# A decoder layer on one core: VectorE forms the second modulation set amid the attention output's tiles

## The chip, the core and the metric

The kernel runs on 1 core of one Trainium2 chip. The metric is the device time of one execution in microseconds (us). TensorE multiplies matrices into PSUM banks, VectorE and ScalarE do elementwise work, GpSimd a little, and SyncE's queue issues nearly all the weight loads; each engine takes its own instructions in order and waits for the others on semaphores.

## The reference

One layer with a mixer (a convolution branch and an attention branch) and a sparse expert stage. What matters here, cut down (D_MODEL is 1024, 256 tokens):

```python
mod = (c_act @ w_ada[l] + b_ada[l])[:, None, :]
shift1, scale1, gate1, shift2, scale2, gate2 = jnp.split(mod, 6, axis=-1)
h = rms_norm(x, norm1_g[l]) * (1.0 + scale1) + shift1
x = x + gate1 * mixer(h, ...)      # q, k, v, conv, gates; attention; w_conv_out, w_attn_out, w_o
h = rms_norm(x, norm2_g[l]) * (1.0 + scale2) + shift2
x = x + gate2 * moe(h, w_router[l], ...)      # top 4 of 32 experts
```

`mod` is one row of 6 x 1024 numbers from a 1024 x 6144 matrix in f32: 24 MB of weights for one row. The experts' weights are 32 x 12 MB.

## The kernel before

**Three modulation sets.** The first set (shift1, scale1) is made at the start. The second (columns 2048 to 4095 of `w_ada`: gate1 and shift2) and the third (scale2 and gate2) are each four blocks of 2 MB, `ADA0[0]` and `ADA0[1]`. The second is formed on TensorE: `ada_rows` (L1267) multiplies all four blocks with the activated `c`, 32 products of 512 columns, each of which the trace shows as two instructions. The third is formed on VectorE: `mod_product(k)` (L885, L887) adds one eighth of the weights, scaled by one number for each partition, to a running sum of 128 x 2048; it starts amid attention head 5 (`MOD_AT`), and `sum_rows` (L1403) on TensorE adds the 128 partitions with four products by ones. `ada_row(gi)` (L877) adds the bias and leaves the row in `modrow2`. ScalarE's queue then sends `modrow2` by 12 small DMAs into `gate1` and `gate2` (inside `u_conv`), spread over the partitions (`mod_ready` counts to 16 x 12). `turn_rows(gi)` (L1393) transposes the row for shift2 or scale2, and VectorE keeps it in `mod2` (L1012, L1094), from which the router's weights are made (L1102 to L1105).

**The ring of weight blocks.** The weights ahead of the experts go through a ring of 6 places (`RING`), 2 MB each. `blocks` lists them in order of loading; block n is loaded by L487 when block n - 6 is used up (`used`). Before the change the order after the first convolution blocks is: second set (4), q and k (4), v (2), gates (4), third set (4), w_conv_out (2), w_attn_out (2), w_o (2).

**The expert slots.** The same memory is 12 slots of 2 MB for the experts: each expert has 6 chunks (4 of `w_up`, 2 of `w_down`), so 12 slots hold two experts. `SLOT_ORDER` says which slot chunk i takes; a slot is free when the mixer's tile or ring block that lay there is done with, and SyncE's stream (L467) waits for each of these ends in turn. Chunks (0,0) to (1,5) are loaded during the mixer and the routing; every later one waits until `chunk_used` tells that expert e - 2 has used its chunk.

**The mixer on TensorE.** In order: the convolution's columns (L1353), the second set (L1267), q and k (8 tiles) and v (4 tiles) at L1361, `turn_rows(0)`, transposes of q and k (L1416), eight heads with the gates' projections between (L1368), `conv_out` 0 to 2, `sum_rows`, transposes of the attention output (L1499), `conv_out(3)`, `turn_rows(1)`, the four tiles of `y_attn` (L1368), the four of `w_o` (L1520), transposes of the new x (L1529), the router, then the expert units. VectorE works on the depthwise convolution (L917, 496 instructions, dealt out between other steps by hand), on q and k, on the heads, and at the end on `y_attn` (L1112, L1114) and in `add_branch` (L1122, L1123), which multiplies a `w_o` tile by `gate1` and adds it to x.

**The four PSUM banks.** `order` numbers the uses of the four banks; use n lies in bank n % 4, and `fill` lets TensorE into it only when VectorE or ScalarE has freed use n - 4.

Of the kernel before, what the change touches and what calls it, by code (L numbers as in the profile page):

```python
# [59 lines left out]
SLOT_ORDER = (HEAD_SLOT, 0, VALUE_SLOT, 1, ROW_SLOT, 2, 3, CONV_SLOT, GATE_SLOT, 4, 5, SMALL_SLOT)  # L60
# [13 lines left out]
def build(nc, x, c, positions, w_ada, b_ada, norm1_g, w_in, conv_w, conv_b, conv_ln_g, conv_ln_b,  # L74
# [3 lines left out]
    with ctx:  # L78
# [28 lines left out]
        def small(shape, dt=F32):  # L107
# [142 lines left out]
        c_ready, ada_done, xT_done = (sem(n) for n in ("c_ready", "ada_done", "xT_done"))  # L250
# [21 lines left out]
        mod_ready, ebias_ready, conv_sum, tables_kept, mod_summed, last_rows, in_cols2 = (  # L272
            sem(n) for n in ("mod_ready", "ebias_ready", "conv_sum", "tables_kept", "mod_summed", "last_rows", "in_cols2"))
# [19 lines left out]
        ADA0 = [len(blocks), 0]  # L293
        blocks += [ada_block(4 * NB, i) for i in range(4)]
# [11 lines left out]
        blocks += [block_of(w_attn_out, 0), block_of(w_attn_out, NB)]  # L306
        WO0 = len(blocks)
# [44 lines left out]
        order += [("ada", 0)] + [("qk", i) for i in range(8)]  # L352
        order += [("v", i) for i in range(4)] + [("mod2T", 0)] + [("qkT", i) for i in range(8)]
# [13 lines left out]
        order += [(name, i) for name in ("y_attn", "w_o") for i in range(4)]  # L367
# [12 lines left out]
        WO_USE = use_of["w_o", 0]  # L380
# [21 lines left out]
        for i in range(3):  # L402
            used[ADA0[0] + i] = (ada_done, i + 1)
            used[ADA0[1] + i] = (mod_summed, 2 * i + 3)
# [5 lines left out]
        for i in range(2):  # L410
# [4 lines left out]
            used_by(WO0 + i, WO_USE + 2 + i)  # L415
# [23 lines left out]
        def _(sp):  # L439
# [34 lines left out]
            for n, src in enumerate(blocks):  # L474
# [15 lines left out]
            sp.wait_ge(*used[COUT0])  # L490
            load_chunk(0, 1)
            full(sp, OT_USE + 3)
            load_chunk(0, 2)
            sp.wait_ge(*used[COUT0 + 1])
            load_chunk(0, 3)
            sp.wait_ge(mod_ready, 16 * 12)
            full(sp, M2T_USE[1])
            sp.wait_ge(ebias_ready, 3 * PARTS)
            load_chunk(0, 4)
            sp.wait_ge(*used[AOUT0])  # L500
            load_chunk(0, 5)
            sp.wait_ge(*used[AOUT0 + 1])
            load_chunk(1, 0)
            full(sp, YA_USE + 3)
            load_chunk(1, 1)
            sp.wait_ge(mixed, 4)
            load_chunk(1, 2)
# [316 lines left out]
        def _(dve):  # L824
# [198 lines left out]
            for h in range(HEADS):  # L1023
# [40 lines left out]
                if h >= MOD_AT:  # L1064
                    mod_product(h - MOD_AT)
# [651 lines left out]
```

## Time and profile before

| | us |
|---|---|
| median of 3 runs | 1262.33 |
| lowest, highest | 1262.19, 1263.87 |
| the profiled execution | 1263.07 |
| its span (first to last instruction) | 1261.2 |
| TensorE busy | 1079.8 (86%) |
| VectorE busy | 417.5 (33%) |
| ScalarE busy | 221.1 (18%) |
| moved by DMA | 475.80 MB, mean 377 GB/s |

The page gives the whole span in 40 slices of 31.5 us. Two stages are to be told apart: up to about 350 us the mixer and the routing, where TensorE is at nine or ten tenths, and from there the experts, where the DMA stream stands at 426 to 429 GB/s. Times "at" in the text are us from the span's start.

### The profile page before, as it was taken

Reading aid. Unit: us, or ns where it says so; the run is one execution under the profiler, and the core shown is the slowest. Engines: PE = TensorE matmul, PEld = TensorE weight load, DVE = VectorE, ACT = ScalarE, POOL = GpSimd, SP = SyncE. Lnnn points to the kernel's source line nnn. Section 1 sums busy time; section 2 is a strip of 40 time slices with the busy share of each in tenths; the row PEclk is TensorE's granted clock in tenths of the full one; section 3 lists DMA queues with packets and bytes.
Section 4 is the critical chain, followed back from the end, with each engine's and each line's share of the span. In section 5 each row is a group of like instructions: output and inputs, shape, how many; then the busy total and the mean of one; then the engine's idle time right before and its main releaser. Section 6 shows DMA issues by size and latency. Waiting matters only on the chain.

```text
span 1261.2 us, 23331 instructions
## 1 busy us (share of the span) xinstructions
PE 1079.8 (86%) x9898; PEld 527.8 (42%) x9898; DVE 417.5 (33%) x1122; ACT 221.1 (18%) x462; POOL 46.0 (4%) x74
## 2 busy tenths in 40 slices
PE   8999999999998766569998668979669696999995
PEld 5864468888442222124443223423224232444431
DVE  1489997762331111113222112312112121223221
ACT  2111133640220101001111001101002111112110
POOL 2000000451000000000000000000000000000000
PEclk9999999999998888889999879979889788999998
DMA  9999353499799999999999999999999999799997
GB/s 329 339 371 361 133 171 134 158 348 347 302 365 428 428 426 427 428 427 428 427 427 428 427 426 429 427 428 427 427 429 426 428 427 428 305 424 428 426 426 321
DMA packets 66491, 475.80 MB, mean 377 GB/s; under 512 B 6417, under 2 KB 20182, under 8 KB 39670
## 3 DMA queue, kind: packets, MB, share of 16 engines
q1 hardware_dynamic: 62676, 472.54, 91.4%
q10 hardware_dynamic: 3746, 2.21, 0.6%
q8 instruction: 58, 0.95, 0.3%
q14 instruction: 11, 0.09, 0.0%
HBM read 473.03 MB, written 1.05 MB: 376 GB/s over the span
## 4 chain that ended last, share of the span: by engine, by line
PE 47%; DMA 31%; SPq 16%; ACT 2%; DVE 2%; issue 1%; another core or an unknown queue 0%; ACTq 0%; DVEq 0%
DMA weights<-in_w_down 25%; SPq L467 15%; PE bank L1651 13%; PE bank L1681 7%; PE bank L1368 7%; PE bank L1361 7%; DMA weights<-in_w_up 4%; PE bank L1297 2%; PE bank L1520 2%; PE bank L1592 2%; DMA weights<-in_w_in 2%; PE bank L1579 2%; PE bank L1353 1%; PE bank L1599 1%; DMA weights<-in_w_ada 1%; ACT buf_d L815 1%
## 5 line engine op out<-in xcount | busy, mean ns | idle before, releaser
L1651 PE MATMUL bank<-weights,buf_d 128*32 128x512 f32 x3008 | 392.8, 669 | 124.7 <-DMA weights<-in_w_up 124.7
L1651 PEld LDWEIGHTS bank<-weights,buf_d 128*32 128x32 f32 x3008 | 96.5, 117 | 388.8 <-DMA weights<-in_w_up 193.0
L1681 PE MATMUL bank<-weights,buf_d 128*32 128x256 f32 x3008 | 185.5, 395 | 42.1 <-DMA weights<-in_w_down 39.2
L1238 DVE TENSOR_SCALAR u_conv<-bank 128x256 f32<-128x256 f32 x47 | 20.0, 425 | 449.2 <-PE bank L1651 449.2
L1681 PEld LDWEIGHTS bank<-weights,buf_d 128*32 128x32 f32 x3008 | 93.2, 113 | 119.1 <-DMA weights<-in_w_down 50.2
L811 ACT ACTIVATE u_conv<-u_conv 128x256 f32<-128x256 f32 x47 | 19.6, 416 | 696.9 <-DVE u_conv L1238 696.9
L917 DVE SCALAR_TENSOR_TENSOR weights<-u_conv,weights 128x256 f32<-128x256 f32 x240 | 97.8, 480 | 0.5
L1361 PE MATMUL bank<-weights,buf_d 128*128 128x512 f32 x192 | 82.7, 593 | 0.1
L1250 DVE TENSOR_TENSOR buf_d<-bank,u_conv 128x256 f32<-128x256 f32 x47 | 20.0, 425 | 187.4 <-PE bank L1681 187.4
L811 ACT ACT_TABLE_LOAD x47 | 60.3, 1283 | 1.4 <-issue 0.6
L1368 PE MATMUL bank<-buf_d,weights 128*128 128x256 f32 x256 | 58.1, 380 | 0.0
L1592 PE MATMUL bank<-buf_d 32*128 32x256 f32 x768 | 57.6, 415 | 0.6 <-DVE buf_d L1250 0.6
L1592 PEld LDWEIGHTS bank<-buf_d 32*128 32x128 f32 x768 | 36.5, 195 | 48.0 <-issue 46.5
L1368 PE MATMUL bank<-weights 128*128 128x256 f32 x256 | 55.9, 379 | 0.0
L1361 PEld LDWEIGHTS bank<-weights,buf_d 128*128 128x128 f32 x192 | 36.4, 190 | 46.4 <-issue 45.4
L1368 PEld LDWEIGHTS bank<-weights 128*128 128x128 f32 x256 | 48.3, 190 | 6.4
L1368 PEld LDWEIGHTS bank<-buf_d,weights 128*128 128x128 f32 x256 | 47.4, 190 | 6.4 <-issue 0.7
L1579 PE MATMUL bank<-x_tok,u_conv 128*32 128x256 f32 x768 | 50.0, 380 | 0.0
L1585 PE MATMUL bank<-ident,buf_d 128*128 128x128 f32 x190 | 38.2, 309 | 0.2 <-ACT buf_d L804 0.2
L1599 PE MATMUL bank<-late,u_conv 96*32 96x256 bf16 (+1 forms) x376 | 34.2, 349 | 0.5 <-DVE buf_d L1200 0.5
L1585 PEld LDWEIGHTS bank<-ident,buf_d 128*128 128x128 f32 x190 | 30.0, 204 | 4.3 <-ACT buf_d L804 0.3
L1199 DVE TENSOR_TENSOR buf_d<-bank,u_conv 128x256 f32<-128x256 f32 x48 | 20.4, 424 | 32.1 <-PE bank L1585 32.1
(276 smaller groups left out, 806.5 us busy)
## 6 DMA issues: line engine op xcount, KB each, us to landing
weights<-in_w_up SPq DMA_DIRECT2D x128, 2048.0 KB, 38.9
weights<-in_w_down SPq DMA_DIRECT2D x63, 2048.0 KB, 44.0
weights<-in_w_in SPq DMA_DIRECT2D x10, 2048.0 KB, 17.5
weights<-in_w_ada SPq DMA_DIRECT2D x8, 2048.0 KB, 13.2
weights<-in_w_ada SPq DMA_DIRECT2D x8, 1024.0 KB, 11.4
weights<-in_w_in SPq DMA_DIRECT2D x8, 512.0 KB, 9.2
weights<-in_w_in SPq DMA_DIRECT2D x4, 1024.0 KB, 13.9
weights<-in_w_conv_out SPq DMA_DIRECT2D x2, 2048.0 KB, 8.0
```

The source lines that it names most:

```text
L467: sp.dma_start(dst, src).then_inc(w_full[chunk_slot(e, j)], 16)
L811: s.activation(sg, glu, ACT.Sigmoid, scale=ALPHA).then_inc(sg_ready, 1)
L917: ins = v.scalar_tensor_tensor(acc, u_conv[:, k, w:w + T], tap(k, w), acc, ALU.mult, ALU.add)
L1297: ins = t.matmul(PS[4 + k][:, T * half:T * half + T], first_conv(i)[:, kk, half, P * k:P * k + P], h1T[:, 2 * i + kk, :], start=False, sto ...
L1361: ins = t.matmul(bank(use)[:, :], lhsT[:, k, P * tt:P * tt + P], blk(n)[:, k, :], start=(k == 0), stop=(k == KD - 1))
L1368: ins = t.matmul(bank(use)[:, T * j:T * j + T], blk(n)[:, k, at:at + P], rhs[:, k, :], start=(k == 0), stop=(k == KD - 1))
L1579: ins = t.matmul(GX[SLOTS * g:SLOTS * g + SLOTS, 0:T], pick[:, tt, :], x_tok[:, tt, T * g:T * g + T], start=(tt == 0), stop=(tt == TT - 1))
L1585: ins = t.transpose(bank_[:, at + P * r:at + P * r + P], src.rearrange("p (c r) -> p r c", r=2)[:, r, :], ident[:])
L1592: ins = t.matmul(Y[q][:, T * tt:T * tt + T], Cmb[rows, P * tt:P * tt + P], oe[rows, :], start=False, stop=True, skip_group_check=True)
L1599: t.matmul(bank_[SLOTS * g:SLOTS * g + SLOTS, 0:width], sel, rows(g), start=True, stop=False)
L1651: ins = t.matmul(UP[SLOTS * g:SLOTS * g + SLOTS, :], xgT[:, r, SLOTS * j:SLOTS * j + SLOTS], up_group(w[:, r, :], g), start=False, stop=(j ...
L1681: ins = t.matmul(DOWN[rows, 0:T], actT[:, r, at:at + SLOTS], w[:, g, r, T * q:T * q + T], start=False, stop=(h == 1 and g == 1 and r == 1))
```

## The change

- TensorE no longer forms the second set: `ada_rows` and the wait for `ada_done` are gone. `mod_product` takes the set as an argument, and VectorE forms the second set too, two products behind each of the four `y_attn` tiles. `sum_rows(0)` comes behind the second `w_o` tile, `turn_rows(0)` behind the third.
- The four blocks of the second set are loaded behind `w_attn_out` and ahead of `w_o`.
- `ada_row(0)`, and with it the 12 small DMAs of `gate1` and `gate2`, comes after the last `y_attn` tile on VectorE; the router's weights are made between the second and the third `add_branch`.
- `SLOT_ORDER` and the waits between the early expert chunks are others; GpSimd's split of the expert biases waits for the second set's last product, no longer the third's.

```diff
-SLOT_ORDER = (HEAD_SLOT, 0, VALUE_SLOT, 1, ROW_SLOT, 2, 3, CONV_SLOT, GATE_SLOT, 4, 5, SMALL_SLOT)
+SLOT_ORDER = (HEAD_SLOT, VALUE_SLOT, 0, 1, 2, CONV_SLOT, GATE_SLOT, 3, 4, ROW_SLOT, 5, SMALL_SLOT)
...
-        ADA0 = [len(blocks), 0]
-        blocks += [ada_block(4 * NB, i) for i in range(4)]
+        ADA0 = [0, 0]
         QK0 = len(blocks)
...
         blocks += [block_of(w_attn_out, 0), block_of(w_attn_out, NB)]
+        ADA0[0] = len(blocks)
+        blocks += [ada_block(4 * NB, i) for i in range(4)]
         WO0 = len(blocks)
...
-        order += [(name, i) for name in ("y_attn", "w_o") for i in range(4)]
+        order += [("y_attn", i) for i in range(4)]
+        order += [("w_o", 0), ("w_o", 1), ("ada", 0), ("w_o", 2), ("mod2T", 0), ("w_o", 3)]
...
+                if n == WO0:
+                    full(sp, OT_USE + 3)
+                    load_chunk(0, 1)
+                    sp.wait_ge(*used[ADA0[0]])
+                    load_chunk(0, 2)
+                if n == WO0 + 1:
+                    sp.wait_ge(*used[ADA0[0] + 1])
+                    load_chunk(0, 3)
                 sp.wait_ge(*used[n - RING])
...
-            pool.wait_ge(mod_summed, KD)
+            pool.wait_ge(mod_summed[0], KD)
...
             glu_tile(7)
-            ada_row(0)
             conv(1, 0, 8)
...
                 v.tensor_tensor(mixT[:, 2 * i:2 * i + 2, :], m, ga, ALU.add).then_inc(mixed, 1)
+                for k in (2 * i, 2 * i + 1):
+                    mod_product(0, k)
+            ada_row(0)
+
+            dve.wait_ge(mod_ready, 16 * 12)
...
+            add_branch(0, 0)
+            add_branch(0, 1)
+            full(dve, M2T_USE[0])
+            v.tensor_copy(by_chunk[:, 0, :, :, :], columns(0, 2)).then_inc(bank_free[M2T_USE[0] % 4], 1)
...
-            fill(pe, ADA_USE[0])
-            for i in range(4):
-                ada_rows(ADA_USE[0], ADA0[0], i)
...
                 ins.then_inc(bank_full[use % 4], 1)
+                if i == 1:
+                    sum_rows(0)
+                if i == 2:
+                    turn_rows(0)
```

What SyncE issues from the second half of w_conv_out on, before (each row a load; `in_w_up` and `in_w_down` are expert chunks):

```order
L487 DMA weights<-in_w_conv_out 128x8x512 [waits bank_full3]
L487 DMA weights<-in_w_attn_out 128x8x512 [waits mod_summed] x2
L487 DMA weights<-in_w_o 128x8x512 [waits mod_summed]
L487 DMA weights<-in_w_o 128x8x512 [waits bank_full3]
L467 DMA weights<-in_w_up 128x4096 [waits bank_full1]
L467 DMA weights<-in_w_up 128x4096 [waits bank_full3]
L467 DMA weights<-in_w_up 128x4096 [waits bank_full0]
L467 DMA weights<-in_w_down 128x4096 [waits ebias_ready,bank_full1,mod_ready]
L467 DMA weights<-in_w_down 128x4096 [waits bank_full3]
L467 DMA weights<-in_w_up 128x4096 [waits bank_full1] x2
L467 DMA weights<-in_w_up 128x4096 [waits mixed]
```

and now:

```order
L498 DMA weights<-in_w_conv_out 128x8x512 [waits bank_full1]
L498 DMA weights<-in_w_attn_out 128x8x512 [waits mod_summed1] x2
L498 DMA weights<-in_w_ada 128x2x2048 [waits mod_summed1]
L498 DMA weights<-in_w_ada 128x2x2048 [waits bank_full1]
L498 DMA weights<-in_w_ada 128x2x2048 [waits bank_full3]
L498 DMA weights<-in_w_ada 128x2x2048 [waits bank_full2]
L470 DMA weights<-in_w_up 128x4096 [waits bank_full1]
L470 DMA weights<-in_w_up 128x4096 [waits mod_summed0]
L498 DMA weights<-in_w_o 128x8x512 [waits bank_full1]
L470 DMA weights<-in_w_up 128x4096 [waits mod_summed0]
L498 DMA weights<-in_w_o 128x8x512 [waits bank_full3]
L470 DMA weights<-in_w_down 128x4096 [waits mod_summed0]
```

Four loads of `w_ada` and three expert chunks now stand ahead of the second load of `w_o`, and the first of `w_o` waits no longer for a product of the third set but for a bank that TensorE fills in `y_attn`.

TensorE from the second `w_o` tile to the transposes of x, before:

```order
L1520 MATMUL bank<-weights,buf_d 128x512 [waits blk_full5,bank_free3]
L1520 MATMUL bank<-weights,buf_d 128x512 x7
L1520 MATMUL bank<-weights,buf_d 128x512 [waits bank_free0]
L1520 MATMUL bank<-weights,buf_d 128x512 x7
L1520 MATMUL bank<-weights,buf_d 128x512 [waits bank_free1]
L1520 MATMUL bank<-weights,buf_d 128x512 x7
L1529 MATMUL bank<-ident,x_tok 128x128 [waits bank_free2]
L1529 MATMUL bank<-ident,x_tok 128x128 x3
```

and now (L1517 is `w_o`, L1401 `sum_rows(0)`, L1391 `turn_rows(0)`, L1530 the transposes of x):

```order
L1517 MATMUL bank<-weights,buf_d 128x512 [waits blk_full5,bank_free1]
L1517 MATMUL bank<-weights,buf_d 128x512 x7
L1401 MATMUL bank<-weights 32x512 [waits mod_summed0,bank_free2]
L1401 MATMUL bank<-weights 32x512 x3
L1517 MATMUL bank<-weights,buf_d 128x512 [waits bank_free3]
L1517 MATMUL bank<-weights,buf_d 128x512 x7
L1391 MATMUL bank<-ident,weights 128x128 [waits bank_free2,bank_free0]
L1391 MATMUL bank<-ident,weights 128x128 x3
L1517 MATMUL bank<-weights,buf_d 128x512 [waits bank_free1]
L1517 MATMUL bank<-weights,buf_d 128x512 x7
L1530 MATMUL bank<-ident,x_tok 128x128 [waits bank_free2]
L1530 MATMUL bank<-ident,x_tok 128x128 x3
```

By the kernel's own list `order`, `turn_rows(0)` has the bank of the first `w_o` tile, and the last `w_o` tile that of the second, so both now stand behind an `add_branch`.

VectorE at the last `y_attn` tile, before (L1112 and L1114 the tile, L1122 and L1123 `add_branch`):

```order
L1112 TENSOR_TENSOR weights<-weights,bank 128x512 [waits bank_full1]
L1114 TENSOR_TENSOR buf_d<-weights 128x512 [waits bank_free1]
L1122 TENSOR_TENSOR bank<-bank,u_conv 128x512 [waits bank_full2,mod_ready]
L1123 TENSOR_TENSOR x_tok<-x_tok,bank 128x512 [waits dve_step]
L1122 TENSOR_TENSOR bank<-bank,u_conv 128x512 [waits bank_full3]
L1123 TENSOR_TENSOR x_tok<-x_tok,bank 128x512 [waits dve_step]
```

and now (L1105 and L1107 the tile, L891 `mod_product`, L883 `ada_row(0)`, L1118 and L1119 `add_branch`):

```order
L1105 TENSOR_TENSOR weights<-weights,bank 128x512 [waits bank_full3]
L1107 TENSOR_TENSOR buf_d<-weights 128x512 [waits bank_free3]
L891 SCALAR_TENSOR_TENSOR weights<-weights 128x2048 [waits mod_summed0,blk_full3]
L891 SCALAR_TENSOR_TENSOR weights<-weights 128x2048 [waits mod_summed0]
L883 TENSOR_TENSOR weights<-bank,weights 128x512 [waits bank_full2,in_rows2]
L1118 TENSOR_TENSOR bank<-bank,u_conv 128x512 [waits bank_full0,mod_ready]
L1119 TENSOR_TENSOR x_tok<-x_tok,bank 128x512 [waits dve_step]
```

Between the last tile and the first `add_branch` two products and the bias row have come in, and the wait for `mod_ready` is now for DMAs that can only start behind that row.

## Rows read from the trace of the kernel before

**Rows 1.** The page, part 2: the DMA rate in 40 slices.
```profile
GB/s 329 339 371 361 133 171 134 158 348 347 302 365 428 428 426 427 428 427 428 427 427 428 427 426 429 427 428 427 427 429 426 428 427 428 305 424 428 426 426 321
```
**Rows 2.** Windows: busy time of each engine, granted clock, DMA share, GB/s.
```profile
core 0: us, PE busy (x) PEld busy (x) DVE busy (x) ACT busy (x) POOL busy (x), PEclk, DMA share, GB/s
345.00:350.00 5.00, 4.04 (x36) 1.94 (x34) 4.30 (x21) 1.93 (x9) 0.00 (x0) 1.00 0.21 39
...
1090.00:1100.00 10.00, 9.94 (x142) 4.88 (x135) 3.03 (x8) 2.72 (x5) 0.00 (x0) 1.00 0.39 165
1100.00:1110.00 10.00, 9.94 (x110) 3.93 (x106) 2.99 (x11) 1.35 (x4) 0.00 (x0) 1.00 0.76 287
```
**Rows 3.** Timeline of SyncE's issues: start, duration, line, tiles, count.
```profile
262.49 11.16 SPq L487 DMA_DIRECT2D weights<-in_w_o  x2
...
337.63 11.24 SPq L467 DMA_DIRECT2D weights<-in_w_down  x2
354.62 5.48 SPq L467 DMA_DIRECT2D weights<-in_w_up  x4
```
**Rows 4.** Timeline of TensorE: start us, us, line, shapes, count.
```profile
80.94 7.07 PE L1267 MATMUL bank<-weights 128*32 128x512 f32 x64
...
187.78 0.52 PE L1425 MATMUL bank<-ident,weights 128*128 128x128 f32 x3
...
272.16 1.06 PE L1403 MATMUL bank<-weights 128*32 128x512 f32 x8
...
309.97 27.63 PE L1520 MATMUL bank<-weights,buf_d 128*128 128x512 f32 x64
...
351.37 8.34 PE L1651 MATMUL bank<-weights,buf_d 128*32 128x512 f32 x64
```
**Rows 5.** Timeline of VectorE from the convolution to the first head.
```profile
86.06 0.42 DVE L892 TENSOR_TENSOR u_conv<-bank,weights 128x256 f32<-128x256 f32 x1
88.15 0.69 DVE L877 TENSOR_TENSOR weights<-bank,weights 128x512 f32<-128x512 f32 x1 [1.67 <-PE bank L1267]
88.76 0.73 DVE L914 TENSOR_SCALAR weights<-u_conv,weights 128x256 f32<-128x256 f32 x2
...
171.41 0.17 DVE L1012 COPY weights<-bank 128x8 f32<-128x8 f32 x1
171.53 8.13 DVE L917 SCALAR_TENSOR_TENSOR weights<-u_conv,weights 128x256 f32<-128x256 f32 x20
...
187.16 0.48 DVE L1044 SCALAR_TENSOR_TENSOR weights<-weights 128x256 f32<-128x256 f32 x1
```
**Rows 6.** Timeline of VectorE: products, bias row, y_attn tiles, add_branch.
```profile
232.34 1.28 DVE L887 TENSOR_SCALAR weights<-weights 128x2048 f32<-128x2048 f32 x1
...
252.69 7.18 DVE L885 SCALAR_TENSOR_TENSOR weights<-weights 128x2048 f32<-128x2048 f32 x3
...
273.37 0.69 DVE L877 TENSOR_TENSOR weights<-bank,weights 128x512 f32<-128x512 f32 x1 [0.22 <-PE bank L1403]
...
296.36 0.69 DVE L1112 TENSOR_TENSOR weights<-weights,bank 128x512 f32<-128x512 f32 x1 [5.42 <-PE bank L1368]
...
310.89 0.69 DVE L1114 TENSOR_TENSOR buf_d<-weights 128x512 f32<-128x512 f32 x1
...
338.44 0.69 DVE L1123 TENSOR_TENSOR x_tok<-x_tok,bank 128x512 f32<-128x512 f32 x1
```
**Rows 7.** Two expert chunks issued at 301.5 and 301.9: issue to landing.
```profile
DMA to landing us min/median/max: 7.7/9.9/12.2
```
**Rows 8.** The 12 small DMAs of modrow2: issue, and issue to landing.
```profile
L613 ACTq DMA_DIRECT2D u_conv<-weights x12: 604/612/635, 275.2 to 282.3; - x12
...
DMA to landing us min/median/max: 5.8/13.4/19.2
```
**Rows 9.** DMA queues from 287 to 290: packets, MB, share (q10 is ScalarE's).
```profile
q1 hardware_dynamic: 83, 1.13, 99.2%
q10 hardware_dynamic: 83, 0.08, 7.9%
```
**Rows 10.** Timeline of TensorE, 16 instructions behind 1.24 and 2.97 us idle.
```profile
397.77 1.93 PE L1651 MATMUL bank<-weights,buf_d 128*32 128x512 f32 x16 [1.24 <-DMA weights<-in_w_up]
402.67 3.64 PE L1651 MATMUL bank<-weights,buf_d 128*32 128x512 f32 x16 [2.97 <-DMA weights<-in_w_up]
```

More of the change, by code:

```diff
@@ L351, in build @@
         order = [("conv", i) for i in range(4, 8)]
[L352 to L353 removed]
+        order += [("qk", i) for i in range(8)]
+        order += [("v", i) for i in range(4)] + [("qkT", i) for i in range(8)]
         for h in range(HEADS):
@@ L379, in build @@
         YA_USE = use_of["y_attn", 0]
-        WO_USE = use_of["w_o", 0]
+        WO_USE = [use_of["w_o", i] for i in range(4)]
         M2T_USE = [use_of["mod2T", i] for i in range(2)]
@@ L402, in build @@
         for i in range(3):
-            used[ADA0[0] + i] = (ada_done, i + 1)
-            used[ADA0[1] + i] = (mod_summed, 2 * i + 3)
+            for gi in range(2):
+                used[ADA0[gi] + i] = (mod_summed[gi], 2 * i + 3)
         for i in (2, 3):
@@ L1095, in _, with add_branch @@
                 bank_free[M2T_USE[1] % 4], 1)
+            dve.wait_ge(gate_ready, 2)
+            for i in range(4):
+                use = YA_USE + i
+                full(dve, use)
+                m = gates[:, 2 * i:2 * i + 2, :]
+                ga = gates[:, KD + 2 * i:KD + 2 * i + 2, :]
+                v.tensor_tensor(ga, ga, bank(use)[:, :].rearrange("p (c t) -> p c t", t=T), ALU.mult).then_inc(bank_free[use % 4], 1)
+                freed(dve, use)
+                v.tensor_tensor(mixT[:, 2 * i:2 * i + 2, :], m, ga, ALU.add).then_inc(mixed, 1)
+                for k in (2 * i, 2 * i + 1):
+                    mod_product(0, k)
+            ada_row(0)
+            dve.wait_ge(mod_ready, 16 * 12)
+            def add_branch(tt, half):
+                use = WO_USE[2 * tt + half]
+                cs = slice(NB * half, NB * half + NB)
+                full(dve, use)
+                step(v.tensor_tensor(bank(use)[:, :], bank(use)[:, :], gate1[:, cs], ALU.mult))
+                v.tensor_tensor(x_tok[:, tt, cs], x_tok[:, tt, cs], bank(use)[:, :], ALU.add).then_inc(bank_free[use % 4], 1)
+            add_branch(0, 0)
+            add_branch(0, 1)
+            full(dve, M2T_USE[0])
+            v.tensor_copy(by_chunk[:, 0, :, :, :], columns(0, 2)).then_inc(bank_free[M2T_USE[0] % 4], 1)
             dve.wait_ge(in_moe, 16)
@@ L1105, in _ @@
             v.tensor_tensor(wr[:], wr[:], mod2[:, 1, :].unsqueeze(2).to_broadcast([P, KD, EXPERTS]), ALU.mult).then_inc(ws_ready, 1)
[L1106 to L1126 removed]
+            add_branch(1, 0)
             dve.wait_ge(h_sq, 3)
@@ L1260, in wait_block @@
                 pe.wait_ge(blk_full[place(n)], 16 * loads_before[n])
-            def ada_rows(use, n0, i):
-                wait_block(n0 + i)
-                for k in (2 * i, 2 * i + 1):
-                    for gi in range(4):
-                        ins = t.matmul(bank(use)[32 * gi:32 * gi + 32, :], c_act[:, k, :], blk(n0 + i, 2)[:, k % 2, NB * gi:NB * gi + NB],
-                                       start=(k == 0), stop=(k == KD - 1))
-                ins.then_inc(*((ada_done, 1) if i < 3 else (bank_full[use % 4], 1)))
             def mod_row(i):
```

101 lines of the change are left out of this document (38 added, 63 removed).

## Prediction, made before the changed kernel was run

> **What bounds the kernel now.** Read the page's second part first, the DMA rate in 40 slices [rows 1]. From the slice at 378 us on nearly all stand at 426 to 429 GB/s, so from there the experts' weights set the pace; before that the rate is far lower, so something else does. The windows and SyncE's timeline tell where the one stage passes into the other. Just before the first unit the DMA does next to nothing (39 GB/s from 345 to 350) [rows 2]: all 12 slots are filled or on their way, the last by the load issued about 348.5, and the next load goes out only at 354.62 [rows 3], when the first expert unit, begun at 351.37 [rows 4], has used its first chunk. From there 180 chunks follow at the DMA's rate. So the end is that moment plus a fixed stream, and every us by which the first unit comes earlier or later is a us of the total. What precedes the first unit is TensorE's chain through the mixer; so I ask how that chain moves.
>
> **Removed from TensorE: 7.07 us, of which 2.5 count.** The 64 instructions at L1267 take 80.94 to 88.0 [rows 4]. They go, and q and k can start at 81. But VectorE is as busy there. Its L892 ends at 86.48; it then waits 1.67 us for TensorE and spends 0.69 us on the bias row, and the next convolution step starts at 88.76 instead of about 86.4 [rows 5]. That is 2.35 us. From there to the first head VectorE is a chain of its own; with the copy at 171.41, which leaves 0.12 us by the starts of two rows [rows 5], its chain gains 2.5 us. It ends the first head's probabilities at 187.64 [rows 5], and TensorE takes them up at 187.78 [rows 4], so the two are level there today. TensorE would be there 7.5 us earlier and must wait about 5 of them. Front: **-2.5 us** (the bound on the other side is -7.5, if VectorE were not in the way).
>
> **Added on VectorE amid y_attn: nothing on the path.** One plain product is 1.28 us, the others 7.18 / 3 = 2.39 [rows 6]; two a tile are at most 4.8, and a tile's own two steps 1.4. VectorE idles 5.42 us ahead of such a tile [rows 6], so a period is 6.9 us and 6.2 are now filled. If the products were 0.7 us dearer, the tiles would slip. The third product ends at 296.36 - 2.5 + 1.4 + 2.4 = 297.7, the fifth 6.9 later at 304.6, the seventh at 311.58 - 2.5 + 2.4 = 311.5, the eighth at 313.9. The blocks themselves are in time: TensorE's use of the conv output and sums lets the last be issued by about 280.
>
> **w_o's weights come late: two waits.** Today both are issued at 262.5 and 273.3, well ahead of 309.97 [rows 3, 4]. Now expert chunk (0,2) waits for the third product (297.7) and the first w_o load stands behind it, at 298.2. Of two loads in a row the second lands 12.2 us after its issue, the first 7.7 [rows 7], so 2 MB more cost about 4.9 with the 0.4 between the issues; w_o's rows are short, and I add 0.4. First w_o block: 298.2 + 12.6 = 310.8. TensorE is there at 309.97 - 2.5 = 307.5, waits 3.3, and the tile (27.63 / 4 = 6.9 [rows 4]) ends at 317.7. The second w_o load needs y_attn's end (307.5), behind chunk (0,3), issued at 304.6: queue 310.8 + 4.8 = 315.6, and 5.4 more gives 321.0. TensorE waits 3.3 again. After idling 2.97 us the granted clock was at its lower level: 16 instructions took 3.64 us instead of 1.93 [rows 10]. I add 1.7 for the second tile (0 to 3.4), and it ends at 321.0 + 6.9 + 1.7 = 329.6; today, less the 2.5, it would end at 321.2. So these waits cost **+8.4 us**.
>
> **gate1 comes late: the largest term.** Then `sum_rows(0)`, 1.06 us [rows 4], the bias row 0.69 [rows 6] and two handovers of 0.1: 331.6. ScalarE issues the 12 small DMAs from 331.8, at 0.61 to 0.64 each [rows 8], the last at 338.9. Landing is the unknown: 5.8 to 19.2 us in the trace [rows 8], with expert chunks in flight then as now. While both queues have work, they move equal numbers of packets, 83 and 83 in 3 us [rows 9], although one queue's are some 14 times as big: a small packet waits its turn behind a chunk's. Here chunks (0,4) to (1,0) go out at about 312, when queued behind w_o land one in some 4.8 us, to 335.4; (1,1) follows `sum_rows` (331) and lands at about 341; (1,2) follows the third w_o tile (338) and lands at about 347. Then the big queue is empty, since (1,3) now waits for `mod_ready`, and the rest of the small packets get through in some 3.5 us. I take **350.5**, nearer to the middle of the landings (338.9 + 11.6) than to either end; the bounds are 338.9 + 5.8 = 344.7 and 338.9 + 19.2 = 358.1.
>
> **Behind it.** Today VectorE handles a w_o tile as soon as TensorE is done, and the last `add_branch` ends at 339.13 [rows 6]. Now nothing is added before 350.7. Two `add_branch` of 1.4 end at 353.6. Only then may TensorE start the last w_o tile, since its bank is that of the second (the order of instructions shows the wait). It has idled some 12 us by then, so it starts at the lower clock: 6.9 + 2.5 (1.3 to 3.4; the first unit of today took 8.34 us for a stage that is 7.0 at the full clock) [rows 4, 10]. It ends at 363.0, and the last `add_branch` at 364.5. The copy for shift2, the router's weights (2.8 us) and the third `add_branch` fit beside that tile. From the last `add_branch` to the first unit the work is today's, 12.2 us (339.13 to 351.37). GpSimd's split of the biases, 24 us from 313.9, ends at about 338 and keeps nobody waiting.
>
> **Sum.** 364.5 - 339.1 = +25.4 us; by parts: -2.5 front, +8.4 w_o's waits, +19.5 for sum, row, DMAs and the last tile behind them. Profiled execution 1263.07 + 25.4 = 1288.5; the median stands 0.7 below that execution, so **1288 us**, 2% slower. Its own range, from the landing's bounds (-6, +7.5) and the clock's (-4, +2.5), mostly not together, is 1281 to 1296.
>
> **Rivals.** *The small DMAs land quickly.* For: some landed within 5.8 us [rows 8]. Against: the median was 13.4. Time: 344.7 instead of 350.5, 1282. The Trainium skill, "DMA: Bandwidth & Descriptors", section on queues, rings and completion order, says that a DMA engine changes from one queue to the next only after a whole packet of some 9 to 17 descriptors. If that held for what the profile counts, the small writes would leave many at a turn and this rival would be the forecast, 1282; the equal counts in the rows speak against it.
>
> *They land slowly.* For: the 12 small DMAs were under way from 275.2 to 282.3 + 19.2 = 301.5, some 26 us [rows 8]. Placed behind 331.8 they end at 358. Against: the chunks run dry at 347 this time. Time: 1288 + 7.5 = 1296.
>
> *TensorE's whole saving counts.* Were VectorE not level with it in the first head, the front would be -7.5, and the total 1283; VectorE's rows speak against it [rows 5].
>
> *The delay is absorbed, and it isn't slower.* Mechanism: the expert stream makes up later what the first unit loses, so that only the front's -2.5 is left: 1260. It needs some 28 us of idle DMA behind the start. The only hole inside is at 1090 to 1110, where 165 and 287 GB/s instead of 428 leave 6.1 + 3.3 = 9.4 us [rows 2], and there TensorE is busy 9.94 of 10 us: it is TensorE's own stretch, which shifts along. The mechanism decides only if the DMA were still filling slots when the first unit starts; it was idle.
>
> **Chances.** Forecast 0.50, quick landing 0.23 (with smaller waits for w_o also below 1281), slow landing 0.14, whole saving 0.09, absorbed 0.04. The forecast's range with most of the two landings gives 1278 to 1297. A change of 0.2% (2.5 us) is about what can be told from none in this kernel. Faster 0.02, within 0.2% 0.02, slower 0.96.
>
> **What would show it.** In the profile of the changed kernel: q and k start at 81; the first head's probabilities are taken up near 185; TensorE idles about 3 us ahead of each of the first two w_o tiles, on `in_w_o`; VectorE's first `add_branch` waits for a DMA of `u_conv` until about 350; the last w_o tile starts behind the second `add_branch`; the first unit starts near 377 and the stream behind it has today's length. It is wrong if the last `add_branch` ends before 355, if the small DMAs land before TensorE is done with the third w_o tile (338), or if the first unit comes late and the end doesn't.

## The result, and the profile after

| | before | after |
|---|---|---|
| median, us | 1262.81 (4 runs, 1262.19 to 1263.87) | 1291.84 (4 runs, 1290.09 to 1293.04) |
| profiled execution, us | 1263.07 | 1292.84 |
| its span, us | 1261.2 | 1290.9 |
| last `add_branch` ends, us from the start | 339.13 | 367.50 |
| first expert unit starts | 351.37 | 379.60 |
| last weight load issued | 1211.91 | 1239.57 |

The kernel became 2.25% slower: the ratio is 1.0225, with a 95% interval from 1.0213 to 1.0237. The forecast was 1288 us with a range of 1278 to 1297. The last three lines of the table tell most of it: 28.4 us are lost before the last `add_branch` and none is given back: at the last weight load 27.7 are left. The remaining 2 us of this execution lie at the very end, where the last piece of `w_down` let TensorE wait 2.85 us instead of 1.34 and the instructions behind it ran at a lower clock; the medians differ by 29.0.

The profile's page, part 2, of the kernel after: the two lines for the granted clock and the DMA rate (40 slices, now of 32.3 us), answers to [rows 1]:

```profile
PEclk9999989998899788879999888988989898999998
...
GB/s 326 335 319 184 173 73 127 222 369 318 348 241 428 428 427 426 428 428 427 427 426 428 427 428 427 428 427 428 425 429 427 426 428 427 316 411 427 426 427 295
```

The reader should see two things. From the 13th slice on the DMA line is the old one: 426 to 429 GB/s, with the same dip near the end. And the slice before it, from 355 us, stands at 241, where the old profile had 365. The windows of the kernel after (columns as in [rows 2]) open up the hole:

```profile
180.00:190.00 10.00, 4.84 (x15) 3.74 (x14) 9.79 (x29) 3.47 (x15) 0.00 (x0) 0.69 0.00 0
190.00:200.00 10.00, 10.00 (x55) 8.24 (x54) 8.27 (x19) 2.92 (x11) 0.00 (x0) 0.97 0.55 210
345.00:350.00 5.00, 0.00 (x0) 0.00 (x0) 0.00 (x0) 0.00 (x0) 0.00 (x0) 0.50 0.91 350
350.00:355.00 5.00, 0.00 (x0) 0.00 (x0) 1.31 (x3) 0.00 (x0) 0.00 (x0) 0.50 0.20 74
```

From 345 to 350 no engine computes, only the DMA works; from 350 to 355 hardly that. The two windows at 180 matter below.

TensorE's timeline of the kernel after, answering to [rows 4] (start, duration, line, shapes, count, and in brackets the idle time ahead with what ended it):

```profile
81.38 19.05 PE L1362 MATMUL bank<-weights,buf_d 128*128 128x512 f32 x44
...
185.76 0.87 PE L1422 MATMUL bank<-ident,weights 128*128 128x128 f32 x3 [5.16 <-DVE weights L1047]
186.43 5.69 PE L1369 MATMUL bank<-buf_d,weights 128*128 128x256 f32 x16
...
282.70 27.79 PE L1369 MATMUL bank<-weights 128*128 128x256 f32 x128
314.70 9.89 PE L1517 MATMUL bank<-weights,buf_d 128*128 128x512 f32 x16 [4.21 <-issue]
325.09 7.10 PE L1517 MATMUL bank<-weights,buf_d 128*128 128x512 f32 x16 [0.49 <-DMA weights<-in_w_o]
332.12 1.06 PE L1401 MATMUL bank<-weights 128*32 128x512 f32 x8
333.12 7.13 PE L1517 MATMUL bank<-weights,buf_d 128*128 128x512 f32 x16
355.13 1.13 PE L1391 MATMUL bank<-ident,weights 128*128 128x128 f32 x4 [14.88 <-DVE x_tok L1119]
356.46 9.51 PE L1517 MATMUL bank<-weights,buf_d 128*128 128x512 f32 x16 [0.20 <-DVE x_tok L1119]
```

And VectorE's, answering to [rows 6], with the 12 small DMAs behind its bias row, answering to [rows 8]:

```profile
303.63 0.69 DVE L1105 TENSOR_TENSOR weights<-weights,bank 128x512 f32<-128x512 f32 x1 [0.85 <-PE bank L1369]
...
311.87 4.73 DVE L891 SCALAR_TENSOR_TENSOR weights<-weights 128x2048 f32<-128x2048 f32 x2
333.33 0.69 DVE L883 TENSOR_TENSOR weights<-bank,weights 128x512 f32<-128x512 f32 x1 [16.73 <-PE bank L1401]
353.65 0.70 DVE L1118 TENSOR_TENSOR bank<-bank,u_conv 128x512 f32<-128x512 f32 x1 [19.63 <-DMA u_conv<-weights]
```
```profile
L620 ACTq DMA_DIRECT2D u_conv<-weights x12: 604/612/630, 334.1 to 341.2; - x12
...
DMA to landing us min/median/max: 7.0/9.4/12.5
```

SyncE's timeline of the kernel after, the two loads of `w_o`, answering to [rows 3]:

```profile
300.81 0.43 SPq L498 DMA_DIRECT2D weights<-in_w_o  x1
...
310.53 0.38 SPq L498 DMA_DIRECT2D weights<-in_w_o  x1
```

Read in order of time, the chain of the loss is all there. TensorE is through with `y_attn` at 310.5, finds no weights and stands for 4.21 us (the profile puts it down to "issue", but the load went out only at 300.81, where it used to go out at 262.5); `sum_rows(0)` comes at 332.12 behind the second `w_o` tile; VectorE, with its products done since 316.6, adds the bias at 333.33; ScalarE sends the row out from 334.1; the first `add_branch` gets it at 353.65; and TensorE, out of work since 340.3, may begin the last `w_o` tile at 356.46, at half clock.

### The profile page after: what moved, and what is told of

It is laid out like the page before. It is cut to its first block, busy times and chain, and to the rows that moved or that the text cites. A ratio compares the mean times of both kernels' runs of the same rounds, so it can differ in the third digit from the quotient of the medians.

```text
span 1290.9 us, 23231 instructions
## 1 busy us (share of the span) xinstructions
PE 1082.4 (84%) x9842; PEld 529.1 (41%) x9842; DVE 432.2 (33%) x1130; ACT 220.0 (17%) x462; POOL 43.7 (3%) x74
## 4 chain that ended last, share of the span: by engine, by line
PE 33%; DMA 30%; SPq 15%; DVE 12%; issue 5%; ACT 3%; ACTq 1%; another core or an unknown queue 0%; DVEq 0%
DMA weights<-in_w_down 24%; SPq L470 15%; PE bank L1652 13%; DVE weights L923 7%; PE bank L1682 7%; DMA weights<-in_w_up 4%; PE bank L1369 3%; PE bank L1298 2%; PE bank L1593 2%; PE bank L1580 1%; DMA u_conv<-weights 1%; DMA weights<-in_w_ada 1%; PE bank L1600 1%; PE bank L1517 1%; ACT buf_d L822 1%
## 5 line engine op out<-in xcount | busy, mean ns | idle before, releaser
L1682 PE MATMUL bank<-weights,buf_d 128*32 128x256 f32 x3008 | 179.8, 386 | 37.5 <-DMA weights<-in_w_down 34.6
L818 ACT ACTIVATE u_conv<-u_conv 128x256 f32<-128x256 f32 x47 | 19.6, 417 | 693.9 <-DVE u_conv L1247 693.9
L1362 PE MATMUL bank<-weights,buf_d 128*128 128x512 f32 x192 | 82.6, 592 | 0.0
L1259 DVE TENSOR_TENSOR buf_d<-bank,u_conv 128x256 f32<-128x256 f32 x47 | 19.9, 424 | 177.1 <-PE bank L1682 177.1
L1593 PE MATMUL bank<-buf_d 32*128 32x256 f32 x768 | 60.3, 431 | 0.6 <-DVE buf_d L1259 0.6
L1517 PE MATMUL bank<-weights,buf_d 128*128 128x512 f32 x64 | 33.6, 686 | 4.9 <-issue 4.2
L891 DVE SCALAR_TENSOR_TENSOR weights<-weights 128x2048 f32<-128x2048 f32 x14 | 33.3, 2381 | 0.3
```

Of the source, the lines that this page charges most:

```text
L818: s.activation(sg, glu, ACT.Sigmoid, scale=ALPHA).then_inc(sg_ready, 1)
L1362: ins = t.matmul(bank(use)[:, :], lhsT[:, k, P * tt:P * tt + P], blk(n)[:, k, :], start=(k == 0), stop=(k == KD - 1))
L1517: ins = t.matmul(bank(use)[:, :], mixT[:, k, P * tt:P * tt + P], blk(n)[:, k, :], start=(k == 0), stop=(k == KD - 1))
L1593: ins = t.matmul(Y[q][:, T * tt:T * tt + T], Cmb[rows, P * tt:P * tt + P], oe[rows, :], start=False, stop=True, skip_group_check=True)
L1682: ins = t.matmul(DOWN[rows, 0:T], actT[:, r, at:at + SLOTS], w[:, g, r, T * q:T * q + T], start=False, stop=(h == 1 and g == 1 and r == 1))
```

## The experiments

All ratios are to the kernel before, run beside it on the same chip. Edits are shown against the changed kernel, that of the front experiment against the kernel before.

**The quiet queue.** Is gate1 late because small DMAs are slow, or because expert chunks are in the way? Here SyncE doesn't load chunks (1,1) and (1,2) until the small DMAs have landed.

```diff
             sp.wait_ge(*used[ADA0[0] + 3])
+            sp.wait_ge(mod_ready, 16 * 12)
             load_chunk(1, 1)
             sp.wait_ge(*used[WO0])
             load_chunk(1, 2)
-            sp.wait_ge(mod_ready, 16 * 12)
```

> The changed kernel, but chunks (1,1) and (1,2) are held back until the 12 small DMAs have landed. Theory: the last small DMA lands some 6 to 7 us after its issue at 341, the first add_branch starts near 348 instead of 353.65, and the total falls by 5 to 6 us, to about 1286.5. Rival (fixed landing time, whatever else is in flight): unchanged, 1291.8.

Measured: 1283.02 us, ratio 1.0152 (1.0135 to 1.0169), against 1.0225 of the change. The landings of the 12 small DMAs and the first `add_branch` in this kernel:

```profile
DMA to landing us min/median/max: 1.9/2.9/4.4
```
```profile
344.56 0.70 DVE L1118 TENSOR_TENSOR bank<-bank,u_conv 128x512 f32<-128x512 f32 x1 [10.77 <-DMA u_conv<-weights]
```

With the same 12 DMAs, issued from 333.9 instead of 334.1 on, the landing falls from 9.4 to 2.9 us in the median, and the first `add_branch` comes 9.1 us sooner. So about 9 us of the change are chunks in the way, more than the 5 to 6 that the theory gave them. What is left of the wait, 10.8 us, is mostly ScalarE's issuing of 12 DMAs at 0.61 each. The chunks held back cost nothing: the first unit starts 9.9 us earlier (369.68), and the span is 9.7 us shorter.

**w_o first.** Both loads of `w_o` are put ahead of the chunks (0,2) and (0,3); the waits for `w_o` should shrink. The rival says that the us won there are lost again on gate1.

```diff
                     load_chunk(0, 1)
-                    sp.wait_ge(*used[ADA0[0]])
-                    load_chunk(0, 2)
-                if n == WO0 + 1:
-                    sp.wait_ge(*used[ADA0[0] + 1])
-                    load_chunk(0, 3)
...
-            sp.wait_ge(*used[ADA0[0] + 2])
-            load_chunk(0, 4)
+            for i in range(3):
+                sp.wait_ge(*used[ADA0[0] + i])
+                load_chunk(0, 2 + i)
```

> The changed kernel, but both w_o loads go out ahead of expert chunks (0,2) and (0,3). The second w_o tile should start about 318 instead of 325.1, 6.9 us earlier. Theory (the small DMAs of gate1 share the queues packet by packet with the expert chunks): the chunks held back are then in flight beside the small DMAs, these still land near 351, and the total falls by 2 to 4 us only, to 1288 to 1290. Rival (the small DMAs take a fixed 12.5 us from their issue): the whole 6.9 us arrive in the total, 1285.

Measured: 1294.98 us, ratio 1.0246 (1.0229 to 1.0263), not faster than the change; whether it is slower, the overlapping intervals don't tell. Both expectations, 1288 to 1290 and 1285, were too low. Its first two `w_o` tiles on TensorE, its first `add_branch`, and its small DMAs:

```profile
310.76 7.03 PE L1513 MATMUL bank<-weights,buf_d 128*128 128x512 f32 x16
318.91 7.11 PE L1513 MATMUL bank<-weights,buf_d 128*128 128x512 f32 x16 [1.13 <-DMA weights<-in_w_o]
```
```profile
356.61 0.70 DVE L1114 TENSOR_TENSOR bank<-bank,u_conv 128x512 f32<-128x512 f32 x1 [28.77 <-DMA u_conv<-weights]
```
```profile
L616 ACTq DMA_DIRECT2D u_conv<-weights x12: 605/612/635, 327.9 to 335.0; - x12
...
DMA to landing us min/median/max: 6.5/14.1/21.6
```

The second tile is over 6.2 us sooner than in the changed kernel and the small DMAs go out 6.2 us sooner, and yet the last one lands 3 us later, 21.6 us after its issue. A wait on the path was removed and another took over its whole length. How the two queues share the DMA can be read off their packets (q1 is SyncE's, q10 ScalarE's), here from 345 to 349 us of this kernel, and then from 343 to 347 of the changed one, where the big queue has gaps up to 345:

```profile
q1 hardware_dynamic: 90, 1.38, 92.7%
q10 hardware_dynamic: 90, 0.13, 9.8%
```
```profile
q1 hardware_dynamic: 72, 0.92, 67.1%
q10 hardware_dynamic: 262, 0.30, 31.7%
```

As in [rows 9], both queues move equal numbers of packets, 90 and 90, while both are full; once the big one has gaps, the small one moves 262 to its 72. So the last small DMA lands at about the time at which the chunks run dry: the last chunk ahead of the first `add_branch`, (1,2), landed at 352.4 us in the changed kernel and at 357.3 here, the last small DMA at 353.7 and 356.6. Why the chunks run dry later here, although (1,2) is issued 6.2 us sooner, the windows tell: with `w_o` first, SyncE holds chunks (0,2) and (0,3) back, and the DMA moves 172 GB/s instead of 317 from 300 to 310 us and 305 instead of 408 from 310 to 320, against 270 instead of 217 from 290 to 300. That is 2.0 MB less, or 4.6 us of stream, and (1,2) lands 4.9 us later. The Trainium skill, "DMA: Bandwidth & Descriptors", section "Queues, rings and completion order", has the engine drain a packet of some 9 to 17 descriptors before it changes to the next queue. The equal counts and the 14.1 us in the median show no such advantage for the queue of small writes; whether what the profile counts as a packet is what that page means by one, no run here shows.

**A warm front.** In the changed kernel TensorE waits 5.16 us ahead of the first head, and the 16 instructions behind it take 5.69 us. Is that the clock, and does it matter? 26 products of constants, whose result nobody reads, fill the gap.

```diff
                 fill(pe, use)
+                if h == 0:
+                    for _ in range(26):
+                        t.matmul(bank(use)[:, 0:384], identb[:], maskb[:], start=True, stop=True, skip_group_check=True)
                 pe.wait_ge(pa_ready, h + 1)
```

> The changed kernel, with 26 idle products of 384 columns in bf16 (some 5 us) in the bank of the first head's transposes, in the 5.16 us that TensorE otherwise idles there. Theory (the front's 2.5 us were lost to the lower granted clock behind that idle time): the projection behind it takes 3.6 us instead of 5.69, y_attn starts near 280 instead of 282.7, total about 1289.0. Rival (something else ate the front's gain): no gain, 1291.8.

Measured: 1287.53 us, ratio 1.0195 (1.0178 to 1.0212). The same place in this kernel, then the 16 instructions in the kernel before (its transposes stand in [rows 4]):

```profile
185.38 0.55 PE L1425 MATMUL bank<-ident,weights 128*128 128x128 f32 x3 [0.80 <-DVE weights L1047]
185.76 3.62 PE L1369 MATMUL bank<-buf_d,weights 128*128 128x256 f32 x16
```
```profile
188.14 3.62 PE L1368 MATMUL bank<-buf_d,weights 128*128 128x256 f32 x16
```

TensorE takes up the first head 2.4 us earlier than before, as forecast, and now keeps them: `y_attn` starts at 279.99, against 282.34 before and 282.70 in the change. So the idle time at the first head did no harm by itself; the clock behind it ate the whole gain of the front. The first unit starts 4.3 us earlier than in the change, 2.7 of that from the front; both loads of `w_o` also land 1.1 us sooner after their issue (why, no run shows), and the last tile takes 8.99 us instead of 9.51.

**Both together.** If the two losses are independent, their gains add.

> The changed kernel with both edits that helped it alone: chunks (1,1) and (1,2) held back until the small DMAs have landed (1283.0), and the 26 idle products in the first head (1287.5 against 1291.8). If the two causes are apart, the gains add: 1283.0 - 4.3 = 1278.7. If they are one, it stays near 1283.

Measured: 1276.68 us, ratio 1.0110 (1.0094 to 1.0125). The ratio is 1.15 points below the change's; the single edits gave 0.73 and 0.30, and their sum is 1.03. The first unit starts at 364.83, 14.8 us earlier than in the change, where the single edits gave 9.9 and 4.3. Within the intervals the gains add, so the two losses are independent.

**gate1 early.** How much is the whole way of gate1 worth, with the bank of the last `w_o` tile? The small DMAs send the memory of the row before it is formed, and VectorE forms `ada_row(0)` behind the wait. So gate1 is not computed; the router then chooses other experts, with other numbers of units, and the total can't be compared, only the time up to the first unit.

```diff
-            for gi in range(2):
-                act_e.wait_ge(bank_free[ADA_USE[gi] % 4], ADA_USE[gi] // 4 + 1)
+            act_e.wait_ge(bank_free[ADA_USE[1] % 4], ADA_USE[1] // 4 + 1)
...
-            ada_row(0)
             dve.wait_ge(mod_ready, 16 * 12)
+            ada_row(0)
```

> The changed kernel with the formed gate1 left out: its 8 DMAs send the bias row alone, as early as before the change, so no add_branch waits for a late DMA; all products, sums and loads stay. Theory (gate1's way through the DMAs, and the last w_o tile behind it, is the largest term): the last w_o tile ends near 347.7 instead of 366, the last add_branch near 349.3 instead of 367.5, total 18 us lower, about 1273.6. Rival (w_o's late weights are the main cost): a fall of under 8 us, above 1284.

Measured: the first unit at 360.81, 18.8 us before the change's (total 1266.77). The waits for `w_o` are untouched, and the last tile starts right behind the third:

```profile
314.14 9.64 PE L1515 MATMUL bank<-weights,buf_d 128*128 128x512 f32 x16 [4.31 <-issue]
324.53 7.11 PE L1515 MATMUL bank<-weights,buf_d 128*128 128x512 f32 x16 [0.76 <-DMA weights<-in_w_o]
...
340.00 7.03 PE L1515 MATMUL bank<-weights,buf_d 128*128 128x512 f32 x16
```

That is the third term of the sum, measured nearly alone: 19.5 in the forecast. Of the 18.8 here 0.6 are already there at the second `w_o` tile (324.53 instead of 325.09); the other 18.2 and the 1.06 us of `sum_rows`, which stays in this kernel, make 19.3.

**The front alone.** In the kernel before, each block of the second set takes one product instead of eight, and nothing else changes. 28 of 32 products are left out, so gate1 and shift2 are wrong, and the router's choices and the number of units with them; only the time up to the first unit is comparable.

```diff
-                for k in (2 * i, 2 * i + 1):
-                    for gi in range(4):
-                        ins = t.matmul(bank(use)[32 * gi:32 * gi + 32, :], c_act[:, k, :], ...)
+                ins = t.matmul(bank(use)[32 * i:32 * i + 32, :], c_act[:, i, :], ...)
```

> The kernel before, with 28 of the 32 products that form the second modulation set left out (4 remain, so that every wait stays); nothing else is moved. Theory (VectorE is level with TensorE in the first head, and the idle time there costs clock): VectorE gains about 1.6 us, TensorE idles some 4 us ahead of the first head's transposes and loses about 2 to the lower clock, total 1262.5 to 1263.8, no gain. Rival 1 (no loss by the clock): about 1261. Rival 2 (the whole 6.2 us count): about 1256.6.

Measured: the first unit at 354.31, 2.9 us later than before (total 1272.32). TensorE behind the products:

```profile
80.89 1.40 PE L1265 MATMUL bank<-weights 128*32 128x512 f32 x8
88.32 11.98 PE L1359 MATMUL bank<-weights,buf_d 128*128 128x512 f32 x21 [6.03 <-DMA weights<-in_w_in]
```

My reason for the front falls in this kernel: it is not VectorE that TensorE waits for, but the weights of q and k, which are loaded behind the four blocks of the second set, the first of them from 67.2 on. The first lands at 88, just as the products used to end. In the changed kernel these loads start at 46.5, and q and k start at 81.38. SyncE's timeline, in the kernel before and in the changed one (from the first block of q and k on):

```profile
67.22 33.13 SPq L487 DMA_DIRECT2D weights<-in_w_in  x6
```
```profile
46.49 21.41 SPq L498 DMA_DIRECT2D weights<-in_w_in  x4
```

So removing the products from TensorE alone gives nothing; it is the other half of the edit, the order of the blocks, that opens the front (no run moves the blocks alone). And behind 6.03 us of idling the 192 instructions of q, k and v take 85.4 us instead of 82.7 (the granted clock is 0.70 and 0.62 in the two windows of 5 us from 85 on), which is nearly all of the 2.9 lost. The theory had VectorE as the reason and the wait at the first head, where this kernel has none.

**The swap.** Must the set with gate1 be the late one? Here gate1 and shift2 are formed amid the heads, and scale2 and gate2, needed only later, amid `y_attn`; gate2 gets four small DMAs and a count of its own.

```diff
-        ADA0[1] = len(blocks)
-        blocks += [ada_block(8 * NB, i) for i in range(4)]
+        ADA0[0] = len(blocks)
+        blocks += [ada_block(4 * NB, i) for i in range(4)]
...
-            ada_row(0)
-
-            dve.wait_ge(mod_ready, 16 * 12)
+
+            dve.wait_ge(mod_ready, 16 * 8)
...
             add_branch(0, 1)
-            full(dve, M2T_USE[0])
+            ada_row(1)
+            full(dve, M2T_USE[1])
```

> The changed kernel with the two late sets exchanged: the set with gate1 is formed amid the heads, the one with scale2 and gate2 amid y_attn, and gate2 has a semaphore of its own. Nothing is left out. Theory (gate1's late arrival is worth some 18 us, w_o's late weights some 8): the last add_branch ends near 349.5, total about 1273.5. Rival (the set's late place itself costs, whatever is in it): above 1285.

Measured: 1274.52 us, ratio 1.0092 (1.0075 to 1.0108), near the theory's 1273.5. gate1's way is gone from the path, the first unit is at 359.51. With `w_o` first on top of it:

> As the exchange of the two sets, and both w_o loads ahead of chunks (0,2) and (0,3). Theory: the two terms add, since no small DMA stands behind w_o any more: 6.9 us below the exchange alone, about 1266.5. Rival (the chunks held back are missed by the first units): no gain over it.

1274.12 us, ratio 1.0082 (1.0065 to 1.0100): the first unit is 4.9 us earlier still, at 354.63, and the total hardly moves, as the rival had it. And with the warm front as well:

> As the exchange with w_o first, plus 26 idle products ahead of the first head's transposes. Theory: a further 2.9 us from the clock, about 1263.5, level with the kernel before. Rival (the front's loss has another cause): no gain over the run without them.

1272.10 us, ratio 1.0073 (1.0056 to 1.0090). Here TensorE's chain is as good as that of the kernel before: the first unit starts at 351.62, against 351.37. The kernel is still 9 us slower, where the theory had it level. So TensorE's chain no longer sets the end. The windows from 0 to 370 us, by the last column, suggest what does; in this order the kernel before, the swap, the swap with `w_o` first, and the same with the warm front:

```profile
0.00:370.00 370.00, 361.58 (x1914) 242.85 (x1918) 229.68 (x572) 96.20 (x231) 45.97 (x74) 1.00 0.77 277
```
```profile
0.00:370.00 370.00, 353.06 (x1752) 239.15 (x1752) 241.94 (x572) 92.82 (x227) 43.72 (x74) 0.98 0.74 267
```
```profile
0.00:370.00 370.00, 355.54 (x1822) 241.82 (x1822) 244.53 (x575) 95.19 (x231) 44.03 (x74) 0.99 0.72 264
```
```profile
0.00:370.00 370.00, 359.33 (x1896) 243.51 (x1900) 246.03 (x580) 95.00 (x231) 43.94 (x74) 1.00 0.74 267
```

Each GB/s of difference over 370 us is 0.37 MB, which the expert stream at 427 GB/s must move later, in 0.87 us.

| kernel | first unit | mean GB/s up to 370 | to move later | expected from that | span, against 1261.2 |
|---|---|---|---|---|---|
| before | 351.37 | 277 | | | |
| swap | 359.51 | 267 | 3.7 MB | +8.7 us | +10.4 |
| swap, w_o first | 354.63 | 264 | 4.8 MB | +11.3 | +13.1 |
| the same, warm front | 351.62 | 267 | 3.7 MB | +8.7 | +8.0 |

The columns agree within 2 us, but that is close to bookkeeping: all these kernels move the same bytes, so what isn't moved by 370 us comes behind it. In the swap alone the first unit, 8.1 us late, would explain the end as well; the other two rows, with the first unit 3.3 and 0.3 us late, are the ones that tell the two bounds apart.

The change takes 8 MB of `w_ada` away from before the stretch in which the DMA has time (133 to 171 GB/s in [rows 1]) and puts them just ahead of the experts, where their chunks want it. The blocks used to be issued from 46 us on; without them the slack stretch begins sooner (from 100 to 120 us the DMA moves 152 GB/s in the changed kernel and 386 in the kernel before). With the DMA at 406 GB/s and more from 320 on in the last two kernels, every MB that isn't loaded by then comes at the end.

**The hole filled.** If that is the bound, a load put where the DMA is idle must shorten the end with TensorE's chain unchanged. In the last kernel the DMA stands at 60 GB/s from 300 to 310 us, because both loads of `w_o` keep chunk (0,2) behind them. Here (0,2) goes between them (the edit is against that kernel).

```diff
                     load_chunk(0, 1)
+                if n == WO0 + 1:
+                    sp.wait_ge(*used[ADA0[1]])
+                    load_chunk(0, 2)
...
-            for i in range(3):
+            for i in (1, 2):
                 sp.wait_ge(*used[ADA0[1] + i])
                 load_chunk(0, 2 + i)
```

> The run with the sets exchanged, w_o first and the idle products, but with chunk (0,2) issued between the two w_o loads, near 298, in the 8 us in which the DMA was nearly idle (60 GB/s from 300 to 310). TensorE's chain up to the first unit is to stay as it was (first unit at 351.6, as in the kernel before). Theory (with 8 MB more to load behind 260 us the DMA is the bound from 308 on, no longer the first unit): one chunk's time or more is won, 5 to 7 us, total 1265 to 1267. Rival (the first unit still sets the end): unchanged, 1272.

Measured: 1266.30 us in 10 runs, ratio 1.0025 (1.0016 to 1.0035), 5.8 us less. The windows at the hole, in the kernel without and with the edit:

```profile
300.00:310.00 10.00, 10.00 (x43) 7.66 (x42) 8.35 (x7) 0.00 (x0) 0.00 (x0) 1.00 0.21 60
```
```profile
300.00:310.00 10.00, 10.00 (x42) 7.79 (x41) 8.21 (x8) 0.00 (x0) 0.00 (x0) 1.00 0.73 278
```

The first unit starts at 351.70 (351.62 without the edit), so TensorE's chain is the same up to there, and the 218 GB/s more over 10 us are 2.2 MB or 5.1 us of stream. The mean up to 370 us is 273 GB/s: 4 below the kernel before, 3.5 us by the rule above, and its span is 4.1 longer. This shows the second bound: the end moved with the bytes while the first unit stood still.

**The sums earlier.** Bringing `sum_rows` one tile ahead might free blocks of the ring sooner.

> As the run with the hole filled, with sum_rows(0) ahead of the third conv output instead of behind it, so that the late set's second block can be loaded some 6 us sooner and the hole from 270 to 280 (303 GB/s) is narrower. Theory (the DMA is the bound): another 2 to 3 us, total about 1263, level with the kernel before. Rival: no difference from the run with the hole filled, or a loss where VectorE is late for the banks.

Measured: 1267.03 us, ratio 1.0031 (1.0019 to 1.0043), no gain. The loads of 270 to 280 do come sooner (398 GB/s instead of 295), but then the DMA stands at 222 from 290 to 300 instead of 403, as the next slots come free no sooner, and TensorE waits for the products: its `w_o` starts 0.9 us later and the first unit 1.2. The mean up to 370 is 272.

Of these kernels none is faster than the kernel before; the best, swap, `w_o` around one chunk, and warm front, is 0.25% slower.

## Why the prediction was right, and where it was off

The range held, and the sum's +25.4 us became +28.4 at the last `add_branch`. Term by term:

| term | forecast | measured | by |
|---|---|---|---|
| front, to the start of `y_attn` | -2.5 | +0.4 | 282.70 against 282.34 |
| waits for `w_o`, to `sum_rows` | +8.4 | +8.0 | 332.12 against 309.97 + 13.8 = 323.8, less the 0.4 |
| gate1's way and the last tile | +19.5 | +20.0 | 28.4 at the last `add_branch`, less the 8.4 |

- **The front was mis-sized, and it is nearly the whole miss of 3.0 us at the last `add_branch`.** The step "TensorE would be there 7.5 us earlier and must wait about 5 of them. Front: -2.5 us" is right in its first half: 5.16 us of idle time, the first head taken up at 185.76, 0.5 us later than forecast. It left out what idling does to the clock, although I charged that for `w_o` from [rows 10]. The granted clock is 0.69 in the window from 180 and 0.97 in the next; transposes took 0.87 us instead of 0.52 and projections 5.69 instead of 3.62. That is 2.4 of the 2.9 us, and the kernel with the warm front gives them back.
- **The products beside `y_attn`** cost nothing, as forecast: with a period of 6.9 us VectorE is idle 0.85 us ahead of a tile where 0.7 were expected. It was close: products dearer by 0.4 us each would have delayed the tiles.
- **The two waits for `w_o`** came out at 8.0 for 8.4, but otherwise distributed. Counted from a front that is 2.9 us later, the first block was due at 313.7 and the tile began at 314.70; the loss by the clock fell into the first tile (9.89 us) and not into the second, which found its weights after only 0.49 us.
- **gate1's way** was right in its mechanism and within 0.5 us in its size, the latter in part by luck. `sum_rows` starts 2.5 us later than forecast (332.12 for 329.6); moved by that, the forecast has the first `add_branch` at 353.2, the trace 353.65. I chose near the median landing of [rows 8], for the reason that chunks end at 347 and small packets get through behind them; the quiet queue (2.9 us) and `w_o` first (14.1) show that this reason, not the median, sets it. But chunk (1,2), issued 2.3 us later than forecast, landed 5.4 us later (352.4 for 347), so 3.1 of them are an error of mine; and the last small DMA landed 1.3 us behind it instead of 3.5. Two errors nearly cancel. *They land quickly* would have needed a nearly empty queue, and then it is 9 us and not the 6 that I gave it: my lower bound of 5.8 us was itself a landing amid chunks. *They land slowly* is what happens when `w_o` is loaded first.
- **The last tile** took 9.51 us (forecast 9.4), behind the second `add_branch` as the order of instructions said.
- **My reason at the front was wrong in one half.** I took VectorE's chain for the only thing that TensorE has to wait for. It is, but only since the weights of q and k are loaded 21 us sooner (46.5 instead of 67.2); without that, TensorE gains nothing.
- ***The delay is absorbed*** did not happen: 28.4 us at the last `add_branch`, 27.7 at the last load. The last 2 us of the profiled execution, a longer wait and a lower clock at its very end, stand in no term of the sum.
- **"A fixed stream follows the first unit"** held for this change because the DMA had run empty before the first unit (74 GB/s from 350 to 355). It is no law: in the kernels with the swap the slots are still being filled then, and the end goes by the bytes that are left. That a second bound lies so close behind the first, I had not seen: one kernel with TensorE's chain as before was still 9 us slower.

## What to carry to other kernels

When loads are moved, do two sums: the chain of the engine that sets the start of the saturated stream, and the bytes that the DMA has moved by then; a load moved out of a stretch with idle DMA costs time later even if the chain is untouched. Here 8 MB, 19.6 us of stream at 427 GB/s, cost 9 us with TensorE's chain as before, and 3 once a hole in the DMA's work was filled. A small transfer on the critical path that starts while large loads are queued lands when these run dry. Holding back loads that weren't urgent gained 9 us here; hurrying the ones ahead of it gained nothing. And an engine that gets work taken away and must wait for another instead is not merely no faster: 5.16 us of idling put TensorE's clock down here, and the stretch behind it must be charged at the lower rate.

## What the runs showed of the hardware

- Small DMAs (32 and 64 KB) landed after 1.9 to 4.4 us in a nearly empty queue and after up to 21.6 us beside 2 MB loads, on a queue of their own. The low end, 1.9 us, is near the fixed cost of about 2.0 us that the Trainium skill gives in "DMA: Bandwidth & Descriptors", section "Anatomy of one DMA", for DMAs that GpSimd issues; these were issued by ScalarE. Beside the chunks the median was 9.4 and more, so there this kernel's time follows the rows and not that figure.
- TensorE's granted clock was at 0.50, its level of 1.2 GHz, in the changed kernel's windows from 345 to 355 us, before which it had been idle for 5 us. After 5.16 us of idling, 16 instructions took 5.69 us instead of 3.62. Products that nobody reads, put into that wait, kept it at 1.00, its level of 2.4 GHz, from 180 to 190 us, and were worth 0.3% of the whole kernel.
